# The softmax's maxima as rows for products of 32, in place of diagonals for products of 128

## The reference

```python
score = einsum('bth,bths->bts', wi, relu(einsum('bthd,bsd->bths', qi, ki_all)))
score = where(allowed, score, -inf)
top_val, top_idx = lax.top_k(score, topk)             # 256 keys of each token
logits = einsum('btngd,btknd->btngk', qg, kg) * HEAD_DIM ** -0.5
p = jax.nn.softmax(where(valid, logits, -inf), axis=-1)   # n = 2 key heads, g = 4 query heads
o = einsum('btngk,btknd->btngd', p, vg)
```

## Time and profile before

| | |
|---|---|
| median of 3 runs without a profile | 3089.64 us (3088.87 to 3091.21) |
| the profiled execution | 3094.46 us, its span 3092.7 us |
| PE busy | 2847.1 us (92%) |
| DVE busy | 1653.3 us (53%) |
| ACT busy | 985.8 us (32%) |
| attention of blocks 0 to 7, layer 0 | 402.6 to 638.1 us |
| the same, layer 1 | 1918.0 to 2153.8 us |

### The profile page before, as it was taken

The page is one execution under the profiler, slowest core; times in us unless marked ns, Lnnn a source line. Parts: engine busy times, 40 slices in busy tenths (PEclk is TensorE's granted clock), DMA queues, the critical chain, the costliest instruction groups (busy, mean ns, idle before and its releaser), DMA issues.

```text
span 3092.7 us, 42630 instructions
## 1 busy us (share of the span) xinstructions
PE 2847.1 (92%) x15994; PEld 2459.7 (80%) x16018; DVE 1653.3 (53%) x2788; ACT 985.8 (32%) x1259; POOL 617.6 (20%) x262
## 2 busy tenths in 40 slices
PE   5999778969999999999979987889999999999996
PEld 2778633349999999999967875333899999999996
DVE  6758766684352443534544778564335435353355
ACT  4246536523221111111233563563332111111112
POOL 1411300001122222222242122000112222222221
PEclk9999889979999999999989998999899999999998
DMA  5412100142122222222241311001112222222222
GB/s 212 134 63 83 35 21 1 38 168 75 66 83 70 82 71 86 80 70 82 70 141 43 116 49 36 1 1 34 56 55 88 70 80 78 72 88 70 80 80 85
DMA packets 71351, 224.93 MB, mean 73 GB/s; under 512 B 17232, under 2 KB 17488, under 8 KB 70096
## 3 DMA queue, kind: packets, MB, share of 16 engines
q1 hardware_dynamic: 69664, 217.26, 21.1%
q10 hardware_dynamic: 1584, 6.29, 0.5%
HBM read 211.44 MB, written 11.54 MB: 72 GB/s over the span
## 4 chain that ended last, share of the span: by engine, by line
issue 46%; PE 36%; DVE 6%; ACT 5%; POOL 4%; DVEq 2%; DMA 1%; ACTq 0%; POOLq 0%; SPq 0%
PE ps L919 33%; ACT notsel L728 4%; POOL w_lo L581 4%; PE ps L965 1%; DVE hf L1311 1%; DMA w_ada<-in_w_ada 1%; DVEq L1436 1%; PE ps L1026 1%; DVE ada_later L1330 1%; DVE ada_junk L1330 0%; PE ps L945 0%; DVE s_cand L1434 0%; DVE swapped L1401 0%; DVEq L1340 0%; PE ps L903 0%
## 5 line engine op out<-in xcount | busy, mean ns | idle before, releaser
L581 POOL TENSOR_TENSOR w_lo<-w_raw,w_hi 128x1024 fp32r<-128x1024 f32 x202 | 498.3, 2467 | 2360.6 <-ACT w_hi L680 2360.6
L919 PE MATMUL ps<-u_hi,w_hi 128*128 128x352 f32 (+1 forms) x2112 | 457.4, 325 | 2.1 <-ACT rstd L872 2.1
L919 PE MATMUL ps<-u_hi,w_lo 128*128 128x352 f32 (+1 forms) x2112 | 458.4, 325 | 0.0
L919 PE MATMUL ps<-u_lo,w_hi 128*128 128x352 f32 (+1 forms) x2112 | 455.7, 324 | 0.0
L680 ACT CAST w_hi<-w_raw 128x1024 fp32r<-128x1024 f32 x202 | 211.0, 1045 | 545.7 <-PE ps L919 336.1
L919 PEld LDWEIGHTS ps<-u_hi,w_hi 128*128 128x128 f32 x2112 | 362.1, 189 | 3.7 <-ACT rstd L872 2.7
L919 PEld LDWEIGHTS ps<-u_hi,w_lo 128*128 128x128 f32 x2112 | 361.0, 189 | 0.0
L919 PEld LDWEIGHTS ps<-u_lo,w_hi 128*128 128x128 f32 x2112 | 361.0, 189 | 0.0
L728 ACT ACTIVATE notsel<-score,s_cand 128x384 bf16<-128x384 f32 (+3 forms) x248 | 297.4, 1200 | 142.2 <-DVE s_cand L1434 141.9
L1741 DVE SCALAR_TENSOR_TENSOR x<-ps,mod,x 128x704 f32 (+2 forms) x240 | 125.4, 578 | 364.5 <-PE ps L919 358.8
L919 PE MATMUL ps<-a_hi,w_hi 128*128 128x352 f32 x1056 | 228.8, 325 | 4.2 <-POOL w_lo L581 2.1
(11 more groups left out here) (260 smaller groups left out, 4122.9 us busy)
## 6 DMA issues: line engine op xcount, KB each, us to landing
w_ada<-in_w_ada SPq DMA_DIRECT2D x96, 512.0 KB, 4.6
w_raw<-in_w_up SPq DMA_DIRECT2D x88, 512.0 KB, 3.5
w_raw<-in_w_in SPq DMA_DIRECT2D x34, 512.0 KB, 3.6
ada_later<-in_w_ada SPq DMA_DIRECT2D x32, 512.0 KB, 3.5
cw<-in_convw SPq DMA_DIRECT2D x32, 512.0 KB, 4.5
w_raw<-in_w_down SPq DMA_DIRECT2D x32, 384.0 KB, 3.1
w_raw<-in_w_down SPq DMA_DIRECT2D x32, 320.0 KB, 2.9
w_raw<-in_w_out SPq DMA_DIRECT2D x16, 512.0 KB, 3.5
```

The source lines that it names most:

```text
L581: nc.gpsimd.tensor_tensor(w_lo[slot][:], w_raw[:], w_hi[slot][:].bitcast(F32), ALU.subtract)\
L919: last = nc.tensor.matmul(ps[:, bank + t, 0:w], wt[slot][:, kk, :], mv[:, kk, t * TW:t * TW + w], start=(kk == 0 and p == 0), stop=(kk == ...
```

## The change

`smax2` becomes 128 tokens by 64 columns: the maximum of key head n and query head b is in column 32 n + b, the other columns are zero (set once at the start). The second key range of a long block goes into `smax_far` and is merged. Once DVE has a block's maxima it raises `mx_ready`, before the last decision of the search. PE has a new unit **T i**, `turn_maxima`: it transposes `smax2` to 64 rows by 128 tokens in a pair of banks of its own turn, so the turns of all later units shift. T 0 stands behind the L units of block 0, T i+1 behind S(i,0) (for i = 0 that is behind pv(0,0) too). DVE's `rows(i+1)`, directly behind `maxima(i+1)`, waits for it and multiplies the transposed maxima, 64 rows, with `minus`, which has -1 at [32 n + b, b] and else zero: `negrow`, 64 rows by 4 x 128, has in row 32 n + b the negated maxima of head b in that head's 128 columns. There are two `negrow`. The subtraction in `st` is then a product of 32 rows for each key head, rows 0 to 31 for n = 0 and 32 to 63 for n = 1. `diagonals` is gone. The sample's part stays as it was.

```diff
+                if kb == 0 and i + 1 < QB:
+                    yield "T", i + 1
...
-        negmax = place("negmax", CS_O, [P, 8, P], F32R)
+        negrow = [place(f"negrow{s}", CS_O + s * 2048, [64, 4, P], F32R) for s in range(2)]
+        negmax = place("negmax", CS_O, [P, 2, P], F32R)
...
+                def turn_maxima(i):
+
+                    pe.wait_ge(mx_ready.sem, mx_ready.at(l, i + 1))
+                    pair_free(("T", i))
+                    nc.tensor.transpose(ps[0:64, PLACE["T", i], 0:P], smax2[:, i % 2, :], ident).then_inc(mx_turned.sem, 1)
...
-                        last = nc.tensor.matmul(ps[:, bank + n, :], ones_r[:], negmax[:, 4 * n:4 * n + 4, :], start=False, stop=True)
+                        r = slice(DEC * n, DEC * (n + 1))
+                        last = nc.tensor.matmul(ps[:, bank + n, :], ones_r[r, :], negrow[i % 2][r, :, :], start=False, stop=True)
...
+                    dve.sem_inc(mx_ready.sem, 1)
                     if i in SEARCH_IN:
                         decide(searched + SEARCH_IN[i], PSRCH, NSRCH)
...
-                def diagonals(i):
-
-                    if i >= 1:
-                        dve.wait_ge(st_ready.sem, st_ready.at(l, i * (i + 1) // 2))
-                    spread(8, smax2[:, i % 2, 0, :])
+                def rows(i):
+
+                    dve.wait_ge(mx_turned.sem, mx_turned.at(l, i + 1))
+                    if i >= 2:
+                        dve.wait_ge(st_ready.sem, st_ready.at(l, (i - 1) * i // 2))
+                    nc.vector.tensor_tensor(negrow[i % 2][:], ps[0:64, PLACE["T", i], 0:P].unsqueeze(1).to_broadcast([64, 4, P]),
+                                            minus[:].unsqueeze(2).to_broadcast([64, 4, P]), ALU.mult).then_inc(nm_ready.sem, 1)
...
                         searched = maxima(i + 1, searched)
+                        rows(i + 1)
                         for _ in range(SEARCH_BESIDE.get(i, 0)):
...
                             dve.drain()
-                        diagonals(i + 1)
```

More of the change, by code:

```diff
@@ L71, with order @@
 N_L, N_S = len(L_UNITS), len(S_UNITS)
-ORDER = [u for i in range(-1, QB) for u in
-         [("L", n) for n, x in enumerate(L_UNITS) if x[0] == i + 1] + [("S", n) for n, x in enumerate(S_UNITS) if x[0] == i]]
+def order():
+    for i in range(-1, QB):
+        yield from (("L", n) for n, u in enumerate(L_UNITS) if u[0] == i + 1)
+        if i < 0:
+            yield "T", 0
+        for n, (block, kb) in enumerate(S_UNITS):
+            if block == i:
+                yield "S", n
+                if kb == 0 and i + 1 < QB:
+                    yield "T", i + 1
+ORDER = list(order())
 PAIRS = (0, 4, 6)
@@ L253, in build @@
         cond_row = small("cond_row", [P, 2, D], F32)
-        smax2 = small("smax2", [P, 2, 2, 8], F32)
+        smax2 = small("smax2", [P, 2, 64], F32)
+        smax_far = small("smax_far", [P, 8], F32)
+        minus = small("minus", [64, 4], F32)
         smax_s = small("smax_s", [P, 2, N_SL + 1], F32)
@@ L371, in build @@
         nm_ready = signal("nm_ready", QB + 1)
+        mx_ready = signal("mx_ready", QB)
+        mx_turned = signal("mx_turned", QB)
         st_ready = signal("st_ready", N_S + N_SS)
@@ L1122, in pair_free @@
                         kind, n = IN_PLACE_BEFORE[unit]
-                        taken = s_taken if kind == "L" else p_ready
+                        taken = {"L": s_taken, "S": p_ready, "T": nm_ready}[kind]
                         pe.wait_ge(taken.sem, taken.at(l, n + 1))
@@ L1170, in _ @@
                 for kind, n in ORDER:
+                    if kind == "T":
+                        turn_maxima(n)
+                        continue
                     if kind == "L":
@@ L1368, in _ @@
             nc.vector.tensor_copy(ones_r[:], ones)
+            nc.vector.memset(smax2[:], 0.0)
+            for n in range(2):
+                r = slice(DEC * n, DEC * (n + 1))
+                nc.vector.tensor_scalar(minus[r, :], ident[r, DEC * n:DEC * n + 4], -1.0, None, ALU.mult)
             for b in range(4):
@@ L1655, in maxima @@
                         bank = PLACE["L", s]
-                        nc.vector.tensor_reduce(smax[:, c // 512, :].rearrange("p (n b) -> p n b", n=2)[:, :, b],
-                                                ps[:, bank:bank + 2, 0:w], AX.X, ALU.max).then_inc(s_taken.sem, 1)
+                        to = smax_far[:] if c else smax
+                        nc.vector.tensor_reduce(to.rearrange("p (n b) -> p n b", n=2)[:, :, b], ps[:, bank:bank + 2, 0:w], AX.X, ALU.max)\
+                            .then_inc(s_taken.sem, 1)
                     dve.drain()
                     if (i + 1) * P > 512:
-                        nc.vector.tensor_tensor(smax[:, 0, :], smax[:, 0, :], smax[:, 1, :], ALU.max)
+                        near = smax.rearrange("p (n b) -> p n b", n=2)[:, :, 0:4]
+                        nc.vector.tensor_tensor(near, near, smax_far[:].rearrange("p (n b) -> p n b", n=2), ALU.max)
                         dve.drain()
+                    dve.sem_inc(mx_ready.sem, 1)
                     if i in SEARCH_IN:
@@ L1687, in _ @@
                 searched = maxima(0, searched)
-                diagonals(0)
+                rows(0)
                 dve.wait_ge(ki_stored.sem, ki_stored.at(l, 16))
```

## The result

The changed kernel takes 3117.74 us (median of 4 runs, 3115.77 to 3121.93), the kernel before 3090.43 beside it (4 runs, 3088.87 to 3093.28). The ratio is 1.009, with an interval of 1.0077 to 1.0102: slower by 27.3 us, where 17.9 was forecast. The direction and the two mechanisms of the forecast hold; a third one, worth some 8 to 10 us, was not in its sum. That the time lies just inside the forecast's range (up to 3118) is luck: that end of the range was set by rival B (3117.6), whose mechanism the trace rules out.

A forecast was written before the change was run, and what follows sets the result against it. Each layer was taken to alternate between a chain part and a part that PE bounds; terms of 8.5 and 9.4 us for the layers made 17.9, and 3107.5 us without a profile, range 3097 to 3118.

The forecast's parts named there:

- the two mechanisms of the forecast: 32-row products lengthen each unit that PE bounds by 0.154 us; the multiply before s_cand lengthens the chain by 0.65 a block.
- rival B: In PE's units: the two 32-row products run one after the other, 0.23 us more in each of 44 units; 3117.6; chance 0.11.
- The products in a PE part: From the first values product to a block's last: 0.154 us more a unit, 2.3 us a layer in blocks 2 to 6.
- C: In PE's units: switching between 128 and 32 rows costs nothing, 37 units give back 0.24 us each; 3092.8; chance 0.10.
- block 7's term: Seven units of block 7 at 0.154 us: 1.1 us, of which only 0.2 counts in layer 0.
- The turned maxima in blocks 1, 2, 4, 5, 6: DVE's multiply between the search's last decision and s_cand delays the chain by 0.65 us a block, 3.25 a layer.
- Block 3: The multiply waits for PE, slowed by half clock, to transpose; block 3's first values product starts 2.5 us later in each layer.
- rival A: Clock stays up in block 3: each layer pays 0.85 instead of 2.5 us and gains 1.7; 3100.8; chance 0.18.
- a block 3 at full clock: Sign in block 3 that the forecast is wrong: PE's granted clock doesn't fall there, as rival A has it.
- D: PE parts shrink, clock stays up in blocks 3 and 6 of both layers, 10.1 us off; 3082.7; chance 0.07.
- Blocks 0 and 1: The transpositions delay block 2's logits by about 0.17 us and a search start by about 0.1; together 0.3 a layer.
- The opposite, one or two more falls for 1.7 each: PE's clock falls to half in one or two more places, 1.7 us each: 3109 to 3111, inside the range, no own chance.

The follow-up runs named there:

- the two filled kernels: Changed kernel and kernel before, each with two unread products added in PE's stops before the first values product of most blocks: 3109.54 and 3089.24 us.
- The doubled multiply: The filled changed kernel with the multiply into negrow made twice in a row, a drain between: 3122.43 us, where the filled changed kernel took 3109.54.
- the late one: For 0.66: 64-row products, late transposition and multiply, filled stops, 3084.28 us; for more falls: changed kernel with only transposition and multiply moved late, 3110.81 us.
- the 128-row variant: The changed kernel with the subtraction as 128-row products again, turned maxima and multiply kept: 3111.71 us, ratio 1.0073.

## Where the prediction was right, and the step that failed

**The products in a PE part: right.** 0.154 us a unit was the forecast. Block 7's seven units make 26.75 - 25.67 = 1.08, which is 0.154 each. In blocks 2 to 6 the PE parts at full clock are 0.16 (block 2, the two filled kernels), 0.40 (block 3), 0.48 (block 4 of layer 1), 0.64 (block 5, the filled kernels) and 0.81 (block 6, the filled kernels) longer: 2.5 against 2.3. The pair runs side by side (486.34, both within 0.49), which rules out B, and the first pv product comes at 0.42 after the pair, as put together from the earlier trace rows. The Trainium skill, TensorE: Matmul & The Clock Gate, Packing small matmuls, has 32-row products in distinct row groups run concurrently; the trace now agrees (0.49 us for both). C is ruled out by the unit of 3.94: its unit, 0.24 shorter, is what the 64-row pair gives and the 32-row pair doesn't. The Trainium skill, TensorEngine Tiling (Array Packing), Key Properties, says that a change of tiling mode drains TensorE. With the 0.10 us of each change alone the prediction had a unit some 0.05 us shorter; the measured unit of 3.94 us fits its sum with the weight loads in the open, and not that one. That most of block 7's term hides in layer 0, as forecast from the earlier trace rows, the trace shows too: DVE's last output comes 3.64 us after the start of the last product with the values in before (641.22 against 637.58) and 2.80 in after, where it now waits for ACT's recip. So 0.24 of the 1.08 counts (forecast 0.2).

```profile
651.76 1.38 DVE L1718 TENSOR_TENSOR mix<-ps,recip 64x512 f32<-64x512 f32 x2 [0.34 <-ACT recip L831]
```

**The turned maxima in blocks 1, 2, 4, 5, 6: right, a little low.** Forecast 0.65 each. Layer 0 has 0.47, 0.71, 0.71, 0.97, 0.71, together 3.57 against 3.25. The doubled multiply and the late one (0.75 and 0.66) show that it is this instruction; the 0.3 more in block 5 they don't explain. That it meets no wait for PE in these blocks holds too: in block 4 the transposition at 509.00 was over before the decision ended.

**Block 3: both prices right, its condition not.** With the fall at its place the chain part took 2.46 more (forecast 2.5); without it, 0.96 more (0.85, as rival A had it). The forecast took the first case, the profiled execution of after had the second in layer 0 and 1.2 more in layer 1. It names a block 3 at full clock as a sign of being wrong, and this sign was there. But A's total was wrong all the same: it gave back 1.7 us of slow clock, and these lay in PE work beside the chain part, where nothing but the one wait already counted hung on them. The forecast itself had priced block 3's fall by the chain; A priced the same microseconds a second time, as if PE were the bound, and D did so with two of its four falls.

**Blocks 0 and 1: 0.17 of 0.3 seen.** Block 1 of before began with 0.7 us of half clock, which hides some of its difference. Between the two filled kernels, which have none there, it is 0.82 (12.21 against 11.39): the multiply's 0.65 and the 0.17 forecast for the transposition. Block 0's own difference is lost in its half clock.

The terms together: 17.9 forecast, 16.3 in blocks 1 to 7 of the profiled executions, 16.9 between the filled kernels. That these lie so close is in part luck: the forecast had 5.0 us for block 3 in the two layers, and without its fall it took 2.2; the other terms came out larger, and the 16.3 and 16.9 hold the 0.84 that block 7 of layer 0 hides behind DVE.

**The step that failed** is a term that the sum put at nothing: it took the clock to fall where it fell before and nowhere else. "The opposite, one or two more falls for 1.7 each" was as far as the prediction went, and this had no chance of its own. In its place the profiled execution had six falls more in PE parts, which cost 10.0 us, and filling PE's stops gave the change 8.2 us back and the kernel before only 1 to 2. The prediction knew what is needed: that a fall follows a stop, that before has six stops a layer and that only one of its falls lies in a PE part. Before's stops ahead of pv(i,0) in blocks 1, 2, 4 and 5 were thus four places a layer in which a fall would cost 1.65 us and didn't happen. The change moves each of them. A rival "the falls spread to the stops that had none", four a layer at 1.65, would have given 13.2 us on top of 17.9: 3120.7. Falls came in six of these eight places in the profiled execution.

**What stays open:** why the falls spread. The length of the stop ahead of pv(i,0) doesn't decide it: before kept its clock behind stops of 3.13, 2.75 and 2.84 us (blocks 2, 4, 5 of layer 0), after lost it behind stops of 2.47 in layer 0, and in layer 1 kept it behind stops of the same length (2.46 and 2.47 in blocks 1, 4 and 6). Here is block 2 of before and of after:

```profile
456.23 1.95 PE L1166 MATMUL ps<-probs,vaug 128*128 128x512 f32 x4 [3.13 <-ACT probs L822]
```

```profile
455.88 2.63 PE L1190 MATMUL ps<-probs,vaug 128*128 128x512 f32 x4 [2.47 <-ACT probs L839]
```

Four products with the values, 1.95 us in the one and 2.63 in the other. The row count isn't the cause (the 128-row variant has the falls), nor is the early transposition alone (the late one has more of them). All the unfilled variants share the transposition as a further small product and a further wait of PE in each block, and a later start of many things by some tenths of a microsecond; which of the two matters no run here tells apart. That the falls come from PE's standing still in these places is shown by the filled kernels; that no others would have come by another way isn't.

## What to carry to other kernels

Where PE stands still before its products and the clock holds, a cost may wait there: when a change moves such stops, count each of them as a possible fall, priced by a fall that the trace does show, and give it a chance of its own. Price a slow stretch by what waited for it: beside a longer chain it is free, in a stretch that PE bounds it counts in full. Look at the row count of the neighbours before giving products fewer rows: here 32 rows between 128-row products cost 0.154 us a unit, and 64 rows beside 64-row ones gained 0.24. And an instruction on a chain that others wait for costs its full length (0.75 us for the second multiply in block 4), even where it replaces a longer one that stood elsewhere.

## What the runs showed of the hardware

- Two products of 32 rows, in rows 0 to 31 and 32 to 63, run side by side (0.49 us for both), and still a unit is 0.154 us longer than with two of 128 rows; the row count changes twice more in it. With 64-row products next to the 64-row q-k products it is 0.24 us shorter.
- Products that nobody reads, 1.7 us of PE in a stop of 2.5, made a kernel 8.2 us faster: the granted clock was 1.00 in a stretch where it was 0.51 without them. In two kernels with 64 rows and the late multiply, unfilled and filled, the difference is 13.8 us (3098.1 and 3084.28). The kernel before, with few falls, gained nothing that can be told.
- A PE part at the granted clock of 0.50 for 3.4 us takes 1.65 us longer (24.43 against 22.78). The kernel before had its falls in the same blocks in both traces and both layers; after had them in partly other blocks in its two traces, and behind stops of the same 2.47 us it had them or not.
